# Prompt attention: one query split per head pair, scores over a head's own 64 rows, and two vector steps moved to POOL and ScalarE

## The reference

```python
s = jnp.einsum('bqhd,bkhd->bhqk', qb, k).astype(jnp.float32) * scale
s = s + cb[..., :, None] - c[..., None, :]
p, _ = softmax_stats(s, kpos[None, :] <= qpos[:, None])
return jnp.einsum('bhqk,bkhd->bqhd', p.astype(v.dtype), v)
```

## Time and profile before

| | us |
|---|---|
| median of 3 runs | 2207.09 |
| lowest, highest | 2201.34, 2208.17 |
| the profiled execution | 2205.07 |
| its span, first to last instruction | 2203.1 |
| TensorE's mean granted clock, share of full | 0.917 |

### The profile page before, as it was taken

How to read it: one execution, slowest core, us unless ns; L and a number is a source line. 1 busy time by engine, 2 the same in 40 slices (tenths; PEclk the granted TensorE clock), 3 DMA queues, 4 the chain that set the end, 5 groups by cost and what they waited for, 6 DMA issues and landing times. The chain is left out here.

```text
span 2203.1 us, 35728 instructions
## 1 busy us (share of the span) xinstructions
PE 1893.5 (86%) x10973; PEld 1638.8 (74%) x10973; DVE 1107.0 (50%) x2524; ACT 944.0 (43%) x1546; POOL 846.7 (38%) x458
## 2 busy tenths in 40 slices
PE   2989898989699999999999956667647889999999
PEld 2767676779687778787787635667547788989897
DVE  3434342511287677787786727777532232424242
ACT  3334243422166667676676635555421231212130
POOL 1222231500036666666666762322222133333332
PEclk8999999989799999999999967777878989999999
DMA  4243424253599889889889742544362265556562
GB/s 152 77 155 114 133 74 155 81 162 125 147 295 320 267 282 320 266 294 312 269 291 300 234 153 91 170 138 128 113 236 98 114 229 229 228 229 264 228 247 100
DMA packets 224813, 430.76 MB, mean 196 GB/s; under 512 B 24041, under 2 KB 81258, under 8 KB 223026
## 3 DMA queue, kind: packets, MB, share of 16 engines
q1 hardware_dynamic: 223826, 427.36, 57.3%
q0 software_dynamic: 864, 2.10, 0.3%
HBM read 394.74 MB, written 121.95 MB: 235 GB/s over the span
## 5 line engine op out<-in xcount | busy, mean ns | idle before, releaser
L822 POOL TENSOR_TENSOR vv_lo<-v_raw,vv_hi 128x1024 fp32r<-128x1024 f32 (+1 forms) x192 | 428.9, 2240 | 227.5 <-ACT vv_hi L884 226.3
L1587 POOL TENSOR_TENSOR w_lo<-w_raw,w_hi 128x2048 fp32r<-128x2048 f32 x40 | 183.9, 4600 | 396.6 <-ACT w_hi L1594 396.6
L876 ACT ACTIVATE kt_hi<-ktp 128x1024 fp32r<-128x1024 f32 (+1 forms) x192 | 186.0, 969 | 172.6 <-PE ktp L1028 172.2
L1028 PE MATMUL ktp<-ident,k_raw 128*128 128x128 f32 x1440 | 203.9, 286 | 40.5 <-DVE kt_lo L902 20.5
L1028 PEld LDWEIGHTS ktp<-ident,k_raw 128*128 128x128 f32 x1440 | 174.4, 147 | 73.9 <-DVE kt_lo L902 24.8
L902 DVE TENSOR_TENSOR kt_lo<-ktp,kt_hi 128x1024 fp32r<-128x1024 f32 (+1 forms) x192 | 219.3, 1142 | 7.5 <-ACT kt_hi L876 7.5
L1044 PE MATMUL s_ps<-kt_hi,q_st 128*128 128x256 f32 (+3 forms) x768 | 211.7, 308 | 1.9 <-DVE mx_parts L934 1.9
L884 ACT ACTIVATE vv_hi<-v_raw 128x1024 fp32r<-128x1024 f32 (+1 forms) x192 | 191.4, 997 | 17.8 <-PE o_ps L1059 10.0
L1044 PE MATMUL s_ps<-kt_lo,q_st 128*128 128x256 f32 (+3 forms) x768 | 195.9, 287 | 0.0
L517 PE MATMUL acc<-w_hi,xn_hi 128*128 128x512 f32 x480 | 190.5, 397 | 1.7 <-DVE lz_neg L407 1.7
L517 PE MATMUL acc<-w_lo,xn_hi 128*128 128x512 f32 x480 | 189.3, 394 | 0.0
(11 more groups left out here) (218 smaller groups left out, 4189.4 us busy)
## 6 DMA issues: line engine op xcount, KB each, us to landing
k_raw<-in_cache_fox_k SPq DMA_DIRECT2D x256, 256.0 KB, 4.8
v_raw<-in_cache_fox_v SPq DMA_DIRECT2D x256, 256.0 KB, 4.2
out_win_kv_sample<-in_cache_win_kv SPq DMA_DIRECT2D x32, 2040.0 KB, 9.5
w_raw<-in_w_in SPq DMA_DIRECT2D x32, 1024.0 KB, 5.7
k_raw<-in_cache_win_kv SPq DMA_DIRECT2D x40, 512.0 KB, 5.4
v_raw<-in_cache_win_kv SPq DMA_DIRECT2D x40, 512.0 KB, 7.1
w_raw<-in_w_up SPq DMA_DIRECT2D x16, 1024.0 KB
w_raw<-in_w_down SPq DMA_DIRECT2D x16, 1024.0 KB
```

The costliest lines, as they stand in the source:

```text
L822: gp.tensor_tensor(vv_lo[:, slot, 0:tiles, :], v_raw[:, i % RAW_RING, 0:tiles, :], vv_hi[:, slot, 0:tiles, :].bitcast(F32), ALU.subtract). ...
L876: act.activation(kt_hi[:, slot, :, 0:n], ktp[:, i % 2, :, 0:n], ACT.Copy).then_inc(k_hi, 1)
L1028: last = pe.transpose(ktp[:, i % 2, q, n * P:(n + 1) * P], k_raw[:, i % RAW_RING, n, q * P:(q + 1) * P], ident[:])
L1587: gp.tensor_tensor(w_lo[:, slot, :], w_raw[:, slot, :], w_hi[:, slot, :].bitcast(F32), ALU.subtract).then_inc(slab_lo_done, 1)
```

## The change

Five edits, all in `attend_prompt`:

1. `q_hi` and `q_lo` lose the index of the head: all 128 rows (both heads) are split together, one set at each of the steps 1 to 4, next to the keys, in place of 64 rows by 2048 at steps 0 and 8. The zeros are no longer written or waited for.
2. A score matmul contracts over the 64 rows of its head, of `q` and of `k` alike.
3. `bias_diag` is computed by POOL in a new stage at steps 0 and 16; DVE only waits for it.
4. The FOX chunk is scaled by ACT (a copy with a scale for each row), 8 behind, in place of DVE.
5. SP's wait ahead of the next queries counts four splits for each pair in place of two.

```diff
@@ -1116,8 +1116,8 @@
-        q_hi = sb("q_hi", [P, 2, SETS, SEQ], F32R)
-        q_lo = sb("q_lo", [P, 2, SETS, SEQ], F32R)
+        q_hi = sb("q_hi", [P, SETS, SEQ], F32R)
+        q_lo = sb("q_lo", [P, SETS, SEQ], F32R)
...
@@ -1239,7 +1239,7 @@
                 load_keys(p + 1)
-                sp.wait_ge(q_split, 2 * p + 2)
+                sp.wait_ge(q_split, SETS * p + SETS)
                 hold(sp)
                 load_queries(p + 1)
...
@@ -1259,11 +1259,6 @@
-            for hh in range(2):
-                other = slice(64 - 64 * hh, 128 - 64 * hh)
-                for x in (q_hi, q_lo):
-                    gp.memset(x[other, hh].bitcast(F32), 0.0).then_inc(zeroed, 1)
-
...
@@ -1276,25 +1271,28 @@
-            stream(gp, PAIRS, CHUNKS, (RECIP_BEHIND, normalise), (0, values_lo))
+            def diagonals(p, i):
+                if i % 16 == 0:
+                    hh = i // 16
+                    gp.wait_ge(bias_in[hh], 16 * (p + 1))
+                    gp.tensor_tensor(bias_diag[:, hh].rearrange("p (t n) -> p t n", n=P), bias[:, hh].rearrange("p (t n) -> p t n", n=P),
+                                     causal[:].unsqueeze(1).to_broadcast([P, Q_TILES, P]), ALU.add).then_inc(bias_done, 1)
+
+            gp.wait_ge(in_small, N_SMALL)
+            stream(gp, PAIRS, CHUNKS, (0, diagonals), (RECIP_BEHIND, normalise), (0, values_lo))
 
         @block.scalar
         def _(act):
             act.wait_ge(c_summed, 1)
             act.activation(neg_c[:], o_ps[0:HEADS, 0, :], ACT.Copy).then_inc(c_copied, 1)
-            act.wait_ge(zeroed, 4)
 
             def split_inputs(p, i):
-                if i in (0, 8):
-                    hh = i // 8
-                    rows = slice(64 * hh, 64 * hh + 64)
-                    act.wait_ge(q_in, 16 * (p + 1))
-                    done(act, scored, at_chunk(p, 16 * hh + 15) - CHUNKS)
-                    act.activation(q_hi[rows, hh], q_raw[rows], ACT.Copy).then_inc(q_split_hi, 1)
                 if 1 <= i <= SETS:
                     s = SET_ORDER[i - 1]
+                    act.wait_ge(q_in, 16 * (p + 1))
                     act.wait_ge(k_in, 16 * (p + 1))
                     done(act, scored, at_chunk(p, 28 + i - 1) - CHUNKS)
+                    act.activation(q_hi[:, s], q_raw[:, s], ACT.Copy).then_inc(q_split_hi, 1)
                     act.activation(k_hi[:, s], k_raw[:, s], ACT.Copy).then_inc(k_split_hi, 1)
...
+            def normalise(p, i):
+                if i % 4:
+                    return
+                x, qt = unit_probs(i), i // 4 % 4
+                act.wait_ge(r_den_done, unit(p, i) + 1)
+                act.activation(x, x, ACT.Copy, scale=r_den[:, FOX, qt:qt + 1]).then_inc(fox_normed, 1)
...
-            stream(act, PAIRS, CHUNKS, (EXP_P_BEHIND, exponentials), (TURN_BEHIND, turns_hi), (COPY_BEHIND, outputs), (0, split_inputs))
+            stream(act, PAIRS, CHUNKS, (EXP_P_BEHIND, exponentials), (NORM_BEHIND, normalise), (TURN_BEHIND, turns_hi), (COPY_BEHIND, outputs), (0, split_inputs))
 
         @block.vector
...
             def split_inputs(p, i):
-                if i in (0, 8):
-                    hh = i // 8
-                    rows = slice(64 * hh, 64 * hh + 64)
-                    ve.wait_ge(q_split_hi, 2 * p + hh + 1)
-                    ve.tensor_tensor(q_lo[rows, hh], q_raw[rows], q_hi[rows, hh].bitcast(F32), ALU.subtract).then_inc(q_split, 1)
                 if 1 <= i <= SETS:
                     s = SET_ORDER[i - 1]
+                    ve.wait_ge(q_split_hi, SETS * p + i)
+                    ve.tensor_tensor(q_lo[:, s], q_raw[:, s], q_hi[:, s].bitcast(F32), ALU.subtract).then_inc(q_split, 1)
...
                 if i % 16 == 0:
-                    ve.wait_ge(bias_in[hh], 16 * (p + 1))
-                    ve.tensor_tensor(bias_diag[:, hh].rearrange("p (t n) -> p t n", n=P), bias[:, hh].rearrange("p (t n) -> p t n", n=P),
-                                     causal[:].unsqueeze(1).to_broadcast([P, Q_TILES, P]), ALU.add).then_inc(bias_done, 1)
                     ve.wait_ge(bias_done, 2 * p + hh + 1)
...
-            def normalise(p, i):
...
-                ve.tensor_scalar(x, x, r_den[:, FOX, qt:qt + 1], None, ALU.mult).then_inc(fox_normed, 1)
...
         @block.tensor
...
-                if i % 16 == 0:
-                    pe.wait_ge(q_split, 2 * p + hh + 1)
                 if i < SETS:
+                    pe.wait_ge(q_split, SETS * p + i + 1)
                     pe.wait_ge(k_split, SETS * p + i + 1)
...
-                    last = pe.matmul(s_ps[:, s, 0:len(tiles) * P], q[:, hh, s, qt * P:(qt + 1) * P], k[:, s, cols], start=(n == 0), stop=(n == 2))
+                    last = pe.matmul(s_ps[:, s, 0:len(tiles) * P], q[rows, s, qt * P:(qt + 1) * P], k[rows, s, cols], start=(n == 0), stop=(n == 2))
```

More of the change, by code:

```diff
@@ L1134, in attend_prompt @@
         o_ps = ps("o_ps3", [P, 2, 512])
-        in_small, c_summed, c_copied, c_stored, zeroed = (sem(n) for n in ("in_small3", "c_summed", "c_copied", "c_stored", "q_zeroed3"))
+        in_small, c_summed, c_copied, c_stored = (sem(n) for n in ("in_small3", "c_summed", "c_copied", "c_stored"))
         q_in, k_in, v_in = sem("p3_q_in"), sem("p3_k_in"), sem("p3_v_in")
@@ L1403, in turns_lo @@
                                  turned_part(pt_hi, i).bitcast(F32), ALU.subtract).then_inc(turned_lo, 1)
-            stream(ve, PAIRS, CHUNKS, (KEEP_BEHIND, keep), (KEEP_BEHIND, maximum), (RECIP_BEHIND, denominators), (NORM_BEHIND, normalise),
+            stream(ve, PAIRS, CHUNKS, (KEEP_BEHIND, keep), (KEEP_BEHIND, maximum), (RECIP_BEHIND, denominators),
                    (LOW_BEHIND, turns_lo), (0, split_inputs))
@@ L1421, in score @@
                 tiles = tiles_of(i)
-                if i % 16 == 0:
-                    pe.wait_ge(q_split, 2 * p + hh + 1)
                 if i < SETS:
+                    pe.wait_ge(q_split, SETS * p + i + 1)
                     pe.wait_ge(k_split, SETS * p + i + 1)
                 done(pe, kept, at_chunk(p, i) - SETS)
-                cols = slice(tiles[0] * P, (tiles[-1] + 1) * P)
+                rows, cols = slice(64 * hh, 64 * hh + 64), slice(tiles[0] * P, (tiles[-1] + 1) * P)
                 for n, (q, k) in enumerate(((q_hi, k_hi), (q_lo, k_hi), (q_hi, k_lo))):
-                    last = pe.matmul(s_ps[:, s, 0:len(tiles) * P], q[:, hh, s, qt * P:(qt + 1) * P], k[:, s, cols], start=(n == 0), stop=(n == 2))
+                    last = pe.matmul(s_ps[:, s, 0:len(tiles) * P], q[rows, s, qt * P:(qt + 1) * P], k[rows, s, cols], start=(n == 0), stop=(n == 2))
                 last.then_inc(scored, 1)
```

## The result

The changed kernel takes 2218.76 us (median of 7 runs, 2213.26 to 2222.44) against 2207.09 (7 runs, 2201.34 to 2208.83). The ratio is 1.0057, with a 95% interval of 1.0043 to 1.0070: slower by 0.6%, where 1.7% faster was forecast.

A forecast was written before the change was run, and what follows sets the result against it. No engine was full; DVE was nearest, and PE idled because DVE was late in a few places. First pair 7.3 us plus three pairs at 10.3 made 38.2 off 2207.1: 2168.9 us, range 2156 to 2183.

The forecast's parts named there:

- 64 rows. I price the matmul itself at nothing: Score matmuls: contracting over 64 rows costs or saves nothing, as 8-row and 128-row matmuls had medians of 392 and 394 ns.
- Rival 3 (the clock): Stretches with PE full: 64 rows lower the granted clock, 72 us more, less 38, so 2241 us, slower; chance 4%.
- Rivals 1, 2 and 4: 1: change of pairs slower, 2178 us, 15%; 2: more comes off, 2157, 15%; 4: another loop replaces the stalls, 2203, 4%.
- rival 2: Whole phase: PE idles less, clock stays higher, change of pairs reaches its upper bound; gain some 50 us, 2157; chance 15%.
- Place D: Start of the second head: DVE's `bias_diag`, stretched beside POOL's `v_lo`, moves to POOL; 4.2 us off per pair, 3.9 to 4.8.
- Place A: Change of pairs: query splits spread over steps 1 to 4; 0.5 us off per pair, bounds -1.2 and 3.8.
- Place B: Step 8: DVE's wait for `q_hi` and its `q_lo` go; 5.2 us off per pair, 4.0 to 5.2, first pair about 3.0.
- Scaling on ACT: FOX scaling moved from DVE to ACT: 0.4 us off per pair, bounds 0 and 1.5, with no new wait for ACT.
- `bias_diag` on POOL: POOL's new stage: takes 1.0 to 1.3 us, DVE waits only for the first, which costs 0.3 us once, bounds 0 and 0.8.

The follow-up runs named there:

- the last version: Kernel before with bias add on POOL, scaling on ACT, 128 rows with zeros, queries split in 64x512 pieces, POOL subtracting head 1's low part: 2167.44 us, ratio 0.981.

## Why the prediction was wrong

**The step that failed is "64 rows. I price the matmul itself at nothing".** The price of the matmul was right within 0.02 us (0.56 and 0.58). What I left out is the weight load ahead of it, which is no longer hidden where the rows change. The term belongs in the sum as 64 changes of rows per pair, and the measured size is 68.3 - 54.2 = 14.1 us per pair, 0.22 us for each, some 53 us in all against the 43 that the rest brought.

The rows I rested on could not show it. The earlier trace rows compares durations, and the gap is in no duration: it lies between starts. The trace of before did hold a sign of it, in the idle column of the weight loads of the same line and in the starts of the matmuls:

```profile
L1059 PEld LDWEIGHTS o_ps<-vn_hi,pt 8*128 8x128 f32 x32 | 5.9, 185 | 11.9 <-issue 11.9
```

```profile
1299.70 0.40 PE L1059 MATMUL o_ps<-vv_lo,pt 128*128 128x512 f32 x1
1300.03 0.49 PE L1059 MATMUL o_ps<-vn_hi,pt 8*128 8x512 f32 x1
```

The loads stood idle 0.37 us each (11.9 over 32), but the price is what the matmuls lost: 0.33 us between starts against 0.23 with equal rows (1471.13 to 1471.36), 0.10. For 256 changes in four pairs that is an estimate of 26 us. It would have brought the forecast from 38 us off to some 12, and not to a loss: behind the transposes at the lower clock a change costs more, 0.31 us (0.61 against 0.30), and for that no row shown of before has a price.

I had a rival on the slower side. *Rival 3 (the clock)* was to lower the clock in the stretches with PE full, and I gave it 4%. In part it came, and with it one of my signs of being wrong, PE full below 1.00. The same 66 matmuls around the weighing, before and in the changed kernel:

```profile
1466.00:1475.90 9.90, 9.90 (x66) 9.11 (x65) 5.70 (x25) 4.76 (x12) 2.27 (x2) 1.00 0.00 0
```

```profile
1472.60:1484.90 12.30, 12.30 (x66) 10.38 (x64) 4.88 (x21) 4.63 (x11) 2.50 (x3) 0.87 0.00 0
1421.30:1438.30 17.00, 17.00 (x56) 11.89 (x56) 11.57 (x51) 9.49 (x25) 9.32 (x5) 0.50 0.62 202
```

They took 2.4 us longer, gaps included, and those of the other head 1.5 (1437.00 to 1448.40, at 0.94): 3.9 of the 14.1 us of a pair, not the 18 that the rival asked for. The last row is a stretch in which PE is recorded as full for 17 us, all of them at the lower level. How the 14.1 us part into gap and clock can only be bounded. At the lower clock the gaps of a chunk are 0.31 and 0.12 us (0.61 against 0.30, 0.34 against 0.22), so the 32 chunks of a pair can lose at most some 13.8 us to them. PE's recorded busy time grew by 63.1 - 45.1 = 18.0 us, so by this estimate 4 or more of these 18 are matmuls that ran at the lower level. What holds the clock down there was not shown. *Rivals 1, 2 and 4* are answered by the run with 128 rows: the other edits gave 43 us, over my 38.2 and under the 50 of rival 2.

**Point by point, with 128 rows:**

- *Place D, 4.2 us (3.9 to 4.8).* `keep` of chunk 16 started 5.37 us after POOL's `v_lo` before (1479.39 to 1484.76); now 0.63:

```profile
1398.92 4.55 POOL L1265 TENSOR_TENSOR v_lo<-v_raw,v_hi 128x2048 fp32r<-128x2048 f32 x1 [2.41 <-ACT v_hi L1300]
1399.04 0.71 ACT L1314 ACTIVATE probs<-probs,r_den 128x512 f32<-128x512 f32 x1
1399.55 0.29 DVE L1369 CUSTOM_DVE_ANT_0 probs<-s_ps,bias_diag 128x128 f32<-128x128 f32 x1
```

  The gain is 4.7, near the upper bound (PE's next transposes gain as much): the scaling that ACT took over, 0.71 us beside it, cost nothing here.
- *Place A, 0.5 us (-1.2 to 3.8).* From the transposes of step 1 to the new pair's first `keep` it was 11.96 us; here, 1418.77 to 1429.22, 10.45. The gain is 1.5. The wait for `q_hi` at step 1 was there, 1.60 us, longer than the 1 us that I gave these waits, and the collision with POOL's scaling at step 2 was there too: that `q_lo` took 1.72 us in place of 0.68.

```profile
1422.75 1.72 DVE L1346 TENSOR_TENSOR q_lo<-q_raw,q_hi 128x512 fp32r<-128x512 f32 x1 [0.61 <-ACT q_hi L1295]
1425.60 0.68 DVE L1346 TENSOR_TENSOR q_lo<-q_raw,q_hi 128x512 fp32r<-128x512 f32 x1
```

- *Place B, 5.2 us.* The period fell by 65.3 - 54.2 = 11.1; less D and A, 4.9 are left for B and the scaling together, where I had 5.6. Read directly, the seven chunks around step 8 took 6.95 us (1432.53 to 1439.48) in place of 12.47, 5.5 less; some 0.6 us was lost elsewhere in the pair.
- *Scaling on ACT, 0.4 us per pair.* The runs with and without it are equal, 2189 and 2188.
- *`bias_diag` on POOL.* It took 1.27 us, and no DVE instruction waited for it save the first, 3.36 us with the load of the bias in it.

## What to carry to other kernels

Before you cut a matmul's contraction rows, look at what runs just ahead of it and behind it on PE: if those use other rows, each change cost some 0.2 us here, about the time of a matmul of 256 columns at the lower clock (0.21), and a matmul with zeros in the unused rows took no longer. At such a place read the distance between starts and the idle time ahead of the weight load, not only durations: a price that lies between instructions is in no mean. When an edit bundles several changes, price and try the one on the busiest engine by itself, for it can eat what the others give; here taking it out turned a loss of 0.6% into a gain of 1.9%, and the last version, with zeros and the reference's results, gained as much.

## What the runs showed of the hardware

- A weight load over 64 rows behind matmuls over 128, or over 128 behind 64, did not start until near the recorded end of the matmul ahead (0.07 to 0.08 us before it): 0.33 us of idle PEld into the scores and 0.22 out of them at the lower clock, and, at the higher, 0.09 to 0.20 us more between starts within and behind scores of 512 columns (0.09 on the way out of them, 1486.19 to 1486.51 in the changed kernel against 1471.36 to 1471.59). With equal rows the load was hidden. The Trainium skill, page "TensorE: Matmul & The Clock Gate", section "The mechanism", says that a weight load overlaps matmuls in flight only where their row groups differ, though it also names loads into a background weight buffer among those that are pulled ahead. Here the load was hidden with the same 128 rows throughout, and was not where 64 of them were shared with the matmul in flight; the measurement decides for these two cases. Disjoint halves one behind the other were not tried.
- The mean granted clock fell with the gaps: 0.82 to 0.91 in a period with 128 rows throughout, 0.67 to 0.70 with two changes per chunk, 0.65 with four; with one per chunk on average it was 0.71, so it isn't in proportion to them. PE's record of busy time went the other way (43 to 46, 63 to 66 and 80 us). That record counts the gap as busy, so a fuller PE was a slower one.
- POOL and DVE excluded each other as in the rows of before, and in this phase of the changed kernel and of the one with 128 rows only DVE's subtractions with two SBUF inputs were stretched (0.68 to 1.43 and 1.72 us); beside the 4.55 us of `v_lo` DVE's `keep` kept its 0.29 us.
